# Splitting three head sums into rounded halves, with the passes and the schedule around them, in a hybrid attention and RWKV-7 layer on one Trainium2 core

## What is computed

```python
h = rmsnorm(x, norm1_g); proj = h @ w_in
att = sliding_window_attention(q, k, v, sinks)           # branch a
kk = hs(k * k_k)                                         # branch r (RWKV-7), heads of 64
kk = kk / jnp.maximum(jnp.sqrt(jnp.sum(kk * kk, axis=-1, keepdims=True)), 1e-12)
S, o = lax.scan(step, S0, ...)                           # state update token by token
mean = jnp.mean(o, axis=-1, keepdims=True)
var = jnp.mean(jnp.square(o - mean), axis=-1, keepdims=True)
on = (o - mean) * lax.rsqrt(var + GN_EPS) * lnx_g + lnx_b
bonus = jnp.sum(rh * kh * r_k, axis=-1, keepdims=True) * vh
rw = (on + bonus) * g
x = x + (sum_b sigmoid(gate_b) * (branch_b @ w_branch[b])) @ w_out
x = x + (silu(h2 @ w_ffn_gate) * (h2 @ w_ffn_up)) @ w_ffn_down
```

## Time and profile before

| | |
|---|---|
| median of 3 runs | 3225.79 us (3223.6 to 3227.06) |
| the profiled execution: its time, its span | 3224.8 us, 3223.0 us |
| TensorE busy | 3155.0 us, 98% |
| VectorE, ScalarE, GpSimd busy | 1664.2, 1020.7, 190.5 us |
| mean granted TensorE clock | 0.995 of full speed |

### The profile page before, as it was taken

One profiled execution on the slowest core, in us unless ns is written; L12 is line 12 of the kernel. 1 busy time (PEld: TensorE's weight loads), 2 busy tenths in 40 slices (PEclk: granted clock), 3 DMA queues, 4 the chain that ended last, 5 costly groups with the idle time before them and its releaser, 6 DMA issues.

```text
span 3223.0 us, 65782 instructions
## 1 busy us (share of the span) xinstructions
PE 3155.0 (98%) x27835; PEld 2652.4 (82%) x27835; DVE 1664.2 (52%) x2822; ACT 1020.7 (32%) x1858; POOL 190.5 (6%) x181
## 2 busy tenths in 40 slices
PE   8999999999999999999999999999999999999997
PEld 6777778877777878877777878998777789999997
DVE  6577554577776673444553265305666525432224
ACT  5444333444443443232221033303333312300001
POOL 0011100011010000100110000001111100000000
PEclk9999999999999999999999999999999999999999
DMA  4455442366666852554444673265334445465556
GB/s 160 151 182 176 151 160 93 105 241 199 206 206 219 269 178 92 171 164 136 143 136 155 193 237 101 89 217 168 125 126 128 135 159 174 144 196 177 177 175 193
DMA packets 269443, 532.27 MB, mean 165 GB/s; under 512 B 34016, under 2 KB 37728, under 8 KB 269152
## 3 DMA queue, kind: packets, MB, share of 16 engines
q1 hardware_dynamic: 269152, 528.07, 50.8%
HBM read 415.97 MB, written 112.08 MB: 164 GB/s over the span
## 4 chain that ended last, share of the span: by engine, by line
PE 90%; DVE 5%; ACT 2%; DMA 2%; issue 1%; SPq 0%; POOL 0%; DVEq 0%; ACTq 0%; POOLq 0%
PE PS L827 77%; PE PS L866 6%; PE PS L924 1%; PE PS L995 1%; PE PS L979 1%; PE PS L1159 1%; DMA y<-xres 1%; DVE wl L1600 1%; DMA wl<-weight_lo 1%; DMA raw<-w 1%; PE PS L914 0%; ACT L1188 0%; PE PS L1173 0%; PE PS L1177 0%; DVE op L2114 0%
## 5 line engine op out<-in xcount | busy, mean ns | idle before, releaser
L827 PE MATMUL PS<-hh,wh 128*128 128x512 f32 x1864 | 765.2, 411 | 1.6 <-ACT gst L1247 1.6
L827 PE MATMUL PS<-hh,wl 128*128 128x512 f32 x1864 | 728.7, 391 | 0.0
L827 PE MATMUL PS<-hl,wh 128*128 128x512 f32 x1864 | 728.2, 391 | 0.0
L1207 ACT ACTIVATE wh<-raw 128x512 fp32r<-128x512 f32 x452 | 283.8, 629 | 474.8 <-PE PS L827 366.7
L827 PEld LDWEIGHTS PS<-hh,wh 128*128 128x128 f32 x1864 | 350.6, 188 | 87.0 <-issue 10.4
L1600 DVE TENSOR_TENSOR wl<-raw,wh 128x512 fp32r<-128x512 f32 x452 | 322.2, 715 | 185.6 <-ACT wh L1207 180.6
L827 PEld LDWEIGHTS PS<-hh,wl 128*128 128x128 f32 x1864 | 350.7, 188 | 76.2
L827 PEld LDWEIGHTS PS<-hl,wh 128*128 128x128 f32 x1864 | 351.2, 188 | 73.7 <-issue 8.1
L827 PE MATMUL PS<-hh_last,wh 128*128 128x272 f32 x1280 | 266.2, 289 | 2.0 <-DVE xres L1732 2.0
L827 PE MATMUL PS<-hl_last,wh 128*128 128x272 f32 x1280 | 264.6, 288 | 0.0
L827 PE MATMUL PS<-hh_last,wl 128*128 128x272 f32 x1280 | 262.8, 286 | 0.0
(11 more groups left out here) (285 smaller groups left out, 4698.0 us busy)
## 6 DMA issues: line engine op xcount, KB each, us to landing
wh<-weight_hi SPq DMA_DIRECT2D x500, 256.0 KB, 2.7
wl<-weight_lo SPq DMA_DIRECT2D x500, 256.0 KB, 3.0
raw<-w SPq DMA_DIRECT2D x186, 512.0 KB, 3.6
weight_hi<-wh SPq DMA_DIRECT2D x164, 256.0 KB, 4.4
weight_lo<-wl SPq DMA_DIRECT2D x164, 256.0 KB, 4.7
raw<-w SPq DMA_DIRECT2D x76, 256.0 KB, 3.4
gate_scratch<-gst SPq DMA_DIRECT2D x48, 256.0 KB, 4.1
gb<-gate_scratch SPq DMA_DIRECT2D x24, 512.0 KB, 4.9
```

The lines of the kernel that those rows point to most:

```text
L827: mm = pe.matmul(PS[:, bank(t) + f, 0:t.cols], wt[:, cols], mov[:, m, (t.half + f) * t.cols:(t.half + f + 1) * t.cols], start=(first and a ...
L1207: act.activation(wh[h % 4][:], src, ACT.Copy).then_inc(hi_done, 1)
```

## The change

Three of the four head sums (`kn`, `bo`, `var`) become two F32R matmuls each that add up in one bank: the 0/1 matrix by a rounded half and by the rest (`head_sum`). The 0/1 matrix goes into a tile of its own, `head`, through a transfer into `q` and a ScalarE copy in the first norm. The mean stays one float32 matmul. The halves are made by new passes: for `kn` ScalarE's `ksh` and VectorE's `ksl`; for `bo` ScalarE's `bh` and VectorE's `bl`; for `var` VectorE squares (`sq`), ScalarE rounds its own square (`vh`, in place of `osq`) and VectorE takes the rest (`vl`). BO is no visit any more; its sum stands at the end of LM, into bank 3, and `bv` moves to S1. LM waits for `xd` and no longer for `bv`. `rwl` moves from GpSimd to VectorE. `Ba` now waits for `atl` only, and `Br` for the tail. The softmax division moves from 0.45 to 0.60 of KG. The visits get other weights (S 1.0 to 1.8, KG 8.0 to 9.5, PV 2.0 to 3.0, LM 5.0 to 4.5, BO gone, VAR 3.0 to 3.5).

```diff
         return self.piece[h - 4][-1] + 2.0 if h >= 4 else (-88.0, -87.0, -84.6, -84.2)[h]
 
 
-FRONT = (("S", 1.0), ("ZA", 1.5), ("KG", 8.0), ("PTR", 3.0), ("PV", 2.0), ("BO", 3.0), ("LM", 5.0),
+FRONT = (("S", 1.8), ("ZA", 1.5), ("KG", 9.5), ("PTR", 3.0), ("PV", 3.0), ("LM", 4.5),
          ("S1", 2.2), ("S2", 2.5), ("S3", 2.0), ("S4", 1.8), ("S5", 2.0), ("S6", 2.0), ("S7", 2.0), ("S8", 1.5))
-TAIL = (("Q0", 2.3), ("SA0", 2.0), ("DO0", 2.2), ("Q1", 2.0), ("SA1", 2.0), ("DO1", 2.0), ("MEAN", 3.0), ("VAR", 3.0))
+TAIL = (("Q0", 2.3), ("SA0", 2.0), ("DO0", 2.2), ("Q1", 2.0), ("SA1", 2.0), ("DO1", 2.0), ("MEAN", 3.0), ("VAR", 3.5))
...
                             yield tile("Br", b, d - 2).last + 2.0
@@ -737,7 +741,8 @@
                     yield -99.0 + 0.5 * k
                     sp.dma_start(xin[:, k, 0:BT], x[:, k, CH:CH + BT]).then_inc(xin_ld[k], 16)
                 yield -93.0
-                sp.dma_start(mat[:], mats[:, 0:M_MEAN]).then_inc(ld, 16)
+                sp.dma_start(mat[:], mats[:, 0:M_HEAD]).then_inc(ld, 16)
+                sp.dma_start(q[:, 0, 0:128], mats[:, M_HEAD]).then_inc(ld, 16)
...
                     elif t.stage == "Ba":
                         mv = (ath, atl)
                         if t.i == 0 and first:
-                            pe.wait_ge(V2, last_pair(b).all("V2"))
-                            pe.wait_ge(A2, last_pair(b).all("A2"))
+                            pe.wait_ge(V, last_pair(b).at("V", "atl"))
                     elif t.stage == "Br":
                         mv = (rwh, rwl)
                         if t.i == 0 and first:
-                            pe.wait_ge(G2, last_pair(b).all("G2"))
+                            pe.wait_ge(A2, last_pair(b).all("A2"))
+                            pe.wait_ge(V2, last_pair(b).all("V2"))
...
+            def head_sum(bank_, n, hi, lo):
+
+                pe.matmul(PS[:, bank_, 0:n], head[:], hi[:].rearrange("p a w -> p (a w)")[:, 0:n], start=True, stop=False)
+                return pe.matmul(PS[:, bank_, 0:n], head[:], lo[:].rearrange("p a w -> p (a w)")[:, 0:n], start=False, stop=True)
...
                 yield pr.t("KG")
-                pe.wait_ge(V, pr.at("V", f"sub{pr.chs[-1]}"))
+                pe.wait_ge(V, pr.at("V", "ksl"))
+                if pr.first:
+                    pe.wait_ge(head_in, 1)
                 step("kn")
-                pe.matmul(PS[:, 4, 0:4 * W], mat[:, M_HEAD], flat(pp), start=True, stop=True).then_inc(Tn, 1)
+                head_sum(4, 4 * W, cch, ktl).then_inc(Tn, 1)
...
-                yield pr.t("BO")
-                pe.wait_ge(G, pr.at("G", "bo2"))
-                step("bo")
-                pe.matmul(PS[:, 4, 0:4 * W], mat[:, M_HEAD], flat(cc), start=True, stop=True).then_inc(Tn, 1)
-
...
                 yield pr.t("LM")
-                pe.wait_ge(V, pr.at("V", "bv"))
+                pe.wait_ge(V, pr.at("V", f"xd{pr.chs[-1]}"))
...
                     mm.then_inc(Tn, 1)
+                pe.wait_ge(V, pr.at("V", "bl"))
+                step("bo")
+                head_sum(3, 4 * W, pph, ccl).then_inc(Tn, 1)
...
+                pe.matmul(PS[:, b0_, 0:4 * W], head[:].bitcast(F32), flat(oo), start=True, stop=True).then_inc(T2, 1)
                 yield pr.t("VAR")
-                pe.wait_ge(A2, pr.at("A2", "osq"))
+                pe.wait_ge(V2, pr.at("V2", "vl"))
                 step("var")
-                pe.matmul(PS[:, b1_, 0:4 * W], mat[:, M_HEAD], flat(oo), start=True, stop=True).then_inc(T2, 1)
+                head_sum(b1_, 4 * W, yoh, ool).then_inc(T2, 1)
...
+                    if b == 0:
+                        act.wait_ge(ld, LDALL)
+                        act.activation(head[:], q[:, 0, 0:128], ACT.Copy).then_inc(head_in, 1)
...
+                act.wait_ge(A, pr.at("A", "ksq"))
+                go("ksh", v4(cch), v4(pp), ACT.Copy)
...
+                yield pr.t("PV", 0.7)
+                act.wait_ge(G, pr.at("G", "bo2"))
+                act.wait_ge(V, pr.at("V", "pc"))
+                go("bh", v4(pph), v4(cc), ACT.Copy)
...
-                go("osq", fl(oo), fl(op), ACT.Square)
+                go("vh", fl(yoh), fl(op), ACT.Square)
```

On VectorE, `ksl`, `bl`, `sq` with `vl`, the moved division, `bv` and `rwl`:

```diff
+                yield pr.t("ZA", 0.2)
+                dve.wait_ge(A, pr.at("A", "ksh"))
+                if pr.before:
+                    dve.wait_ge(G, pr.before.at("G", "lb"))
+                tt_("ksl", fl_(ktl), fl_(pp), fl_(cch), ALU.subtract)
...
-                yield pr.t("KG", 0.45)
+                yield pr.t("KG", 0.60)
...
-                yield pr.t("BO", 0.2)
+                yield pr.t("PV", 0.85)
                 dve.wait_ge(Tn, pr.at("T", "x"))
                 if pr.before:
                     dve.wait_ge(V2, pr.before.at("V2", "on"))
                 for c in pr.chs:
                     tt_(f"xd{c}", xd[c][:], q8(3 + 3 * c), mrep(M_XD, 4, c0=0, c1=64), ALU.mult)
-                yield pr.t("BO", 0.4)
-                dve.wait_ge(Tn, pr.at("T", "bo"))
-                own("ktO")
-                tt_("bv", v4(kt), q4(4, W), xs(8), ALU.mult)
-
+                yield pr.t("PV", 0.95)
+                dve.wait_ge(A, pr.at("A", "bh"))
+                tt_("bl", fl_(ccl), fl_(cc), fl_(pph), ALU.subtract)
...
-                    dve.wait_ge(G2, pr.before.all("G2"))
+                    dve.wait_ge(V2, pr.before.all("V2"))
...
+                yield pr.t("S1", 0.3)
+                dve.wait_ge(Tn, pr.at("T", "bo"))
+                tt_("bv", v4(kt), q4(3, W), xs(8), ALU.mult)
...
+                own("oc")
+                tt_("sq", fl_(oo), fl_(op), fl_(op), ALU.mult)
+                dve.wait_ge(A2, pr.at("A2", "vh"))
+                own("sq")
+                tt_("vl", fl_(ool), fl_(oo), fl_(yoh), ALU.subtract)
...
+                yield pr.t("VAR", 0.99)
+                dve.wait_ge(A2, pr.at("A2", "rwh"))
+                tt_("rwl", rwl[:, :, pr.c0:pr.c0 + W], v4(op), rwh[:, :, pr.c0:pr.c0 + W], ALU.subtract)
```

More of the change, by code:

```diff
@@ L241, in steps @@
         s = by("mx") + ["mx2"] + by("sub") + ["msk"] * (first or sample) + ["sk"]
-        s += ["n1", "zp"] + ["lwm"] * sample + ["scan", "sum", "den", "rec", "pn", "kt1", "kt2"] + ["ktm"] * sample
+        s += ["ksl", "n1", "zp"] + ["lwm"] * sample + ["scan", "sum", "den", "rec", "pn", "kt1", "kt2"] + ["ktm"] * sample
         s += ["bb"] + ["bbm"] * sample
-        s += ["at", "rt", "pc", "btE", "btO", "ktE", "ktO", "atl", "xd0"] + ["xd1"] * (not sample) + ["bv"]
-        s += each("lmO", "ydE", "ydO") + ["pt1E1", "pt1O1"] * (not sample) + each("lmE")
+        s += ["at", "rt", "pc", "btE", "btO", "ktE", "ktO", "atl", "xd0"] + ["xd1"] * (not sample) + ["bl"]
+        s += each("lmO", "ydE", "ydO") + ["pt1E1", "pt1O1"] * (not sample) + each("lmE") + ["bv"]
         s += ["yoE1", "yoO1"] * (not sample)
@@ L444, in hybrid_layer @@
         hw0, ha0, hka = (new(n, [128, 4]) for n in ("hw0", "ha0", "hka"))
-        mat = new("mat", [128, M_MEAN, 128])
+        mat = new("mat", [128, M_HEAD, 128])
+        head = new("head", [128, 128], F32R)
         lora = new("lora", [128, 2, 512])
@@ L473, in hybrid_layer @@
         vtk, gg = both_lm[:, :, 0, 0:2, CH:128], both_lm[:, :, 1, :, CH:128]
+        cch, pph = (place(f"{n}h", [128, 4, 128], at_s + i * 2048, F32R) for n, i in (("cc", 4), ("pp", 5)))
+        ktl, ccl = (place(f"{n}l", [128, 4, 128], at_s + i * 2048, F32R) for n, i in (("kt", 7), ("cc", 4)))
+        yoh, ool = (place(n, [128, 4, 128], at_y + i * 2048, F32R) for n, i in (("yoh", 1), ("ool", 2)))
         op, oo = place("op", [128, 4, 128], at_y), place("oo", [128, 4, 128], at_y + 4096)
@@ L708, in gates_in @@
                                 p = last_pair(b)
-                                for s, e in ((V2, "V2"), (A2, "A2"), (G2, "G2"), (T2, "T2")):
+                                for s, e in ((V2, "V2"), (A2, "A2"), (T2, "T2")):
                                     sp.wait_ge(s, p.all(e))
@@ L1524, in fronts @@
                     yield from front(pr)
-            def tails():
-                for pr in pairs:
-                    yield from tail(pr)
             def front(pr):
@@ L1578, in front @@
                 step.end()
-            def tail(pr):
-                step = Order(pr, "G2")
-                W = pr.w
-                yield pr.t("VAR", 0.95)
-                pool.wait_ge(A2, pr.at("A2", "rwh"))
-                out = op[:].rearrange("p a w -> p (a w)")[:, 0:4 * W].rearrange("p (a w) -> p a w", a=4)
-                step("rwl")
-                pool.tensor_tensor(rwl[:, :, pr.c0:pr.c0 + W], out, rwh[:, :, pr.c0:pr.c0 + W], ALU.subtract).then_inc(G2, 1)
-                step.end()
             pool.wait_ge(ld, LDALL)
-            run(leads(), fronts(), tails())
+            run(leads(), fronts())
         @block.vector
@@ L2157, in tail @@
                 tt_("on", fl_(op), fl_(op), fl_(oo), ALU.mult)
+                yield pr.t("VAR", 0.9)
                 own("on")
```

34 lines of the change are left out of this document (15 added, 19 removed).

## The result

The changed kernel takes 3238.05 us in the median (3233.71 to 3239.78, 7 runs) against 3225.79 before: the ratio is 1.0035, 95% interval 1.0026 to 1.0044. It is slower by 0.35%, where I had forecast 25 us less. The profiled execution took 3238.45 us, its span is 3236.7, 13.7 more than before.

The account below looks back on a forecast made before the run. TensorE, busy 98% of the span, was taken as the bound. Terms -19.8, -4.7, -2.0, -1.7, -1.8, -3.1, +3.1, +1, +1, +3 sum to -25.0 us: 3225.8 to about 3200, range 3190 to 3213.

Parts of the forecast that it names:

- shorter waits: TensorE's waits elsewhere: wider S -2.0 us, LM waiting for `xd` instead of `bv` -1.7, copies of `sa` ahead of division -1.8.
- pairs 1 and 2 of block 0: VectorE bounds these pairs, so the `sv` wait moves from DO1 to the mean, with a low-clock stretch: +3.1 us.
- Both signs: Prediction wrong if TensorE's idle time outside the start grows over 6 us, or busy time doesn't fall by about 20.
- rival A: VectorE late for a sum (`ksl`, `bl`) or masked scores, some 0.7 us per pair: 3212 (3206 to 3219), chance 0.17.
- E: Rival, slower: bonus sum at LM's end waits 2.5 us per pair for `bl` behind `bo2` and `bh`: 3241, chance 0.04.
- LM and `xd`: LM waited 1.7 us (`kt`) for `bv`; now it waits for `xd`, two steps earlier on VectorE: -1.7 us.
- The sums: Three head sums per pair as two F32R matmuls instead of plain float32, 0.40 us saved each: -19.8 us.
- Pair 0: First pair's transposes: the 3.0 us wait for `sm` and the 1.7 us low-clock loss behind it vanish: -4.7 us.
- The end of block 0: `Ba` no longer waits 2.9 us for `rwh`, its 1.7 us clock loss goes, some 1.5 us stays at `Br`: -3.1.
- S: Visit S grows from 1.0 to 1.8; of ZA's waits for `sm` and `both_lm`, 2.5 us in all, 2.0 go: -2.0.
- X: Visit X and its masked copies: two passes stand ahead of the keys on VectorE, +1 us.
- rival B: VectorE passes stretched beside GpSimd, one 1.15 us collision per pair: 3219; chance 0.05 beyond forecast's range; sign: mean `wl` above 0.9.

Follow-up runs that it names:

- e1: Changed kernel with the softmax division back at 0.45 of KG, ahead of the copies of `sa`: 3221.83 us, ratio 0.9988 to the kernel before.
- e3: Changed kernel with `bl` directly behind `xd` on VectorE (0.88 of PV, not 0.95), ahead of `lg`, `ob`, `gate`: 3229.15 us, ratio 1.0012 to before.
- e9: e4 with the second keys, `atl`, `xd` and `bl` on VectorE and ScalarE's `bh` earlier within PV: 3205.61 us, ratio 0.9932 to before.
- e2: Changed kernel with each of the three split sums as one float32 matmul over the rounded half, rests made but unused: 3251.51 us, ratio 1.0083 to before.
- e11: e9 with the three split sums again as one float32 matmul over the rounded half: 3221.35 us, ratio 0.9989 to before.
- e10: e4 with `Ba` waiting for the whole tail again instead of `atl`: 3217.84 us, ratio 0.9970 to before.
- e8: e4 with visit S at its earlier weight, 1.0 instead of 1.8: 3216.52 us, ratio 0.9973 to before.
- e4: Changed kernel with both orders mended, division at 0.45 of KG and `bl` at 0.88 of PV: 3213.32 us, ratio 0.9965 to before.

## Why the prediction was wrong, step by step

**The step that failed** is the one on shorter waits: the copies of `sa` now stand ahead of the division and go, -1.8, and in the same breath LM now waits for `xd`, "two steps earlier on VectorE", -1.7. Both took the wait away and did not ask what is late next, outside pairs 1 and 2 of block 0. I had the mechanism in hand there (the division moves in front of `oo`, the wait moves from DO1 to the mean, with the low clock behind it), and priced it at +3.1 for two pairs, since in pair 3 the mean waited only 0.21. But that 0.21 was measured with the division elsewhere. Four passes, 2.9 us together, put into a chain with little slack can make `oo` late in any pair. Measured: 13.8 us in nine pairs. The two pairs of the +3.1 have 4.9 of it (3.3 and 1.65, where I had about 4 and 2.7), so the mechanism was right there and the sum had nothing for the 8.9 in seven others. The removal gives 16.2 (e1), 8.1 of it waits in the trace and most of the rest the clock, while the `sv` waits that it saved are 5.8, of which 4.3 come back. With the 7.2 at the bonus sum and the 7.3 for `xd`, 23.4 us of waits were not in the sum, which missed by 39 (25 less forecast, 14 more measured in the profiled execution). Both signs that I had named for a wrong prediction are there: idle time outside the start grew by 24.0, and busy time fell by 10.6 and not by 20.

**The bonus sum at LM's end** was rival A's and E's place, and I gave it less than 0.3 us. I noted `lg`, `ob` and `gate` as moved behind `xd`, and did not count them between `xd` and `bl`. These three and `bl` itself are 2.7 us behind `xd`, the masked scores 2.06, which gives the 0.6 at once. Measured: 7.2 us of waits, 8.9 in the time (e3).

**LM and `xd`:** forecast -1.7. The waits for `kt` (1.7) are gone, and 7.3 for `xd` have come. It is the distance in the queue that changed: the visit that was taken out had been cover. e9 gives it back for 7.7 us.

**The sums:** forecast -19.8, measured 0.40 to 0.41 in every start to start, 19.6 in sum, and 19.1 to 21.5 in e2 and e11. Right; that some of it would return as waits was not in the sum.

**Pair 0:** forecast -4.7, and the transposes wait no more. But the chain behind them is VectorE's, not the transposes': `ptk` on ScalarE, queued behind VectorE's `ra`, ran at 149.48 in place of 148.97, and PV now waits 2.4 us for it with 6.8 us at the low clock. The wait moved by one visit. The products behind this pair's masked scores run 1.6 us earlier against those ahead of `kn`, and 0.8 of that are two sums: of the 4.7 us, 0.8 came. The chain also holds two stretched passes, `kt` at 142.39 (1.78) and `aa` at 146.40 (1.79), each beside a GpSimd product.

**The end of block 0:** forecast -3.1 with 1.5 us left at Br. Left are 2.2, for another reason: `gst` stands behind `rwh` and a table load on ScalarE (e10: 1 to 2 us of gain).

**S:** forecast -2.0; both waits are gone, and e8 (3.2 slower, not certain) does not speak against the size. **X:** forecast +1, `bkk` waits 2.1 in place of 0.3. **The start:** forecast +1, the first products run 0.3 to 0.5 later. **The products:** forecast +3; the products wait 4.3 more for `gst` and 1.6 more for VectorE's sequencer (`DVEq`).

**The stretched passes (rival B):** not by its sign, and yet in part. VectorE's busy time grew by 49 us for 85 passes of 0.69, 9 less than their sum; passes of a 128x512 subtraction or product above 0.95 us are 27, before 33; and the mean `wl` fell from 0.715 to 0.705, where I had asked for 0.9. But a mean over the whole program does not see where the stretched passes lie: of passes that stood there before, more now lie on the way to `oo` (up to 5.4 of the 13.8 us, above). The Trainium skill's rule ("SBUF — State Buffer", the two separate sides) says that a VectorE pass with two operands in SBUF and a GpSimd instruction that reads SBUF share ports, that the one that starts first keeps them for its whole length, and that the other stands still; the trace agrees, with `aa` at 0.68 when it starts first and at 1.76 when GpSimd's 1.59 does.

**The clock** was in the sum as a term of single places. In the traces it is a term for the whole: ten stretches in the changed kernel, two in e4 and e9, each 1.7 us of TensorE's work, so 14 us between kernels whose waits differ by 12 to 19. The timed runs show less of it. By the mean granted clocks changed and e4 differ by 0.0018, some 6 us of work. And over 151 timed runs, each against the mean of its kernel and session, 0.001 less clock goes with 1.4 us more time, where the lost work is 3.2. So one stretch comes to some 0.8 us in the time on average, an estimate from these slopes; why it isn't 1.7 was not tried.

## What to carry to other kernels

When a step is moved in an in-order queue, the wait that it caused is not the price of its old place: look for the idle time that it filled, and for the next step behind its new place that another engine waits for, in every repetition of the pattern and not only where it is bound already. A visit that is merged into another had been cover for the steps queued beside it, so all distances from a result to its consumer have to be set anew. And the gain of a cheaper step is to be taken from start to start, but a part of it comes back as waits (1.3 of 21.5 and 5.5 of 19.1 us here), as long as the engines that feed it aren't moved with it. Last, a mean duration over the whole program says nothing of the few passes that lie in front of a wait: look at those one by one.

## What the runs showed of the hardware

A wait of TensorE of a given length need not be followed by a stretch at the low clock. The wait of 3.0 us for `fl` in block 2 is there in the changed kernel, in e4, e9 and e10. In the changed kernel the clock falls 1.0 us before its end, in e10 1.6 behind it; in e9 and e4 it does not fall. Of e9, the view of stretches behind its waits of 2.4, 2.2, 2.8 and 3.0 us:

```profile
149.60:153.00 3.40, 3.07 (x46) 2.18 (x47) 3.30 (x6) 2.06 (x4) 0.00 (x0) 1.00 0.91 336
428.40:431.80 3.40, 3.40 (x10) 2.66 (x9) 1.99 (x4) 1.45 (x3) 0.00 (x0) 0.50 0.90 277
653.90:657.30 3.40, 3.36 (x12) 2.98 (x13) 2.52 (x5) 0.37 (x2) 0.00 (x0) 0.53 1.05 334
1457.60:1461.00 3.40, 3.40 (x15) 2.83 (x16) 2.42 (x4) 0.00 (x0) 0.00 (x0) 1.00 0.17 45
```

The longest of the four, 3.0 us, kept the full clock, and that of 2.2 us lost it. Nor is a short wait safe, as I had read from the kernel before (1.3 us and less): the wait of 1.36 us for `gst` at 284.55 in the changed kernel has a stretch that begins 0.15 us behind its end, the same wait of 1.36 in e1 and e9 has none. So one cannot name the price of a single wait of 1.4 to 3 us in advance: it is its length, or its length and up to 1.7 us. The timed runs of one kernel spread by 2 to 8 us, and the clock is a part of that: over the 151 runs time and granted clock correlate with -0.56, so that the clock goes with about a third of the variance.
